# Two joined transformer-style blocks in float32 on one core: SBUF tiles moved to 2048-byte offsets, the compression's position column merged into its matmuls, and all weights packed in the order in which they are loaded

## What is computed

```python
def compress(t, j):                      # keys (j = 0) and values (j = 1)
    blk = t[:, win_idx] + pe[j][None, None, :, None, :]     # 15 windows of 32 tokens, stride 16
    h = jax.nn.silu(jnp.einsum('bnlgd,ldf->bngf', blk, w1[j]))   # l = 32, d = 64, f = 128
    return h @ w2[j]
```

## Time and profile before

| | |
|---|---|
| median of the runs | 2589.13 us (2587.99 to 2589.91, 3 runs) |
| the profiled execution, its own time | 2592.49 us |
| its span | 2590.7 us |
| mean granted TensorE clock | 0.948 |
| PE busy (matmul / weight load) | 2344.5 us (90%) / 1926.3 us (74%) |
| DVE, ACT busy | 1672.1 us (65%), 1098.6 us (42%) |
| transfers | 531.24 MB, 205 GB/s over the span; 208080 of 293659 packets under 2 KB |

### The profile page before, as it was taken

One profiled execution on the slowest core, in us unless ns is written; L12 is line 12 of the kernel. 1 busy time (PEld: TensorE's weight loads), 2 busy tenths in 40 slices (PEclk: granted clock), 3 DMA queues, 4 the chain that ended last, 5 costly groups with the idle time before them and its releaser, 6 DMA issues.

```text
span 2590.7 us, 30688 instructions
## 1 busy us (share of the span) xinstructions
PE 2344.5 (90%) x11132; PEld 1926.3 (74%) x11132; DVE 1672.1 (65%) x2111; ACT 1098.6 (42%) x1221; POOL 0.2 (0%) x4
## 2 busy tenths in 40 slices
PE   0999994899999985999999898999999989899998
PEld 0787884688788774788788686778878869677786
DVE  7677667676677776676677644577757764456444
ACT  1434634433534554443433434543444343464333
POOL 0000000000000000000000000000000000000000
PEclk9999997999999995999999987999999998799999
DMA  9787431497488540596588632248758883223552
GB/s 376 273 299 280 142 109 33 160 322 264 173 321 311 185 163 16 203 321 235 211 319 301 186 115 82 98 166 322 281 187 306 307 239 107 98 98 114 178 194 105
DMA packets 293659, 531.24 MB, mean 205 GB/s; under 512 B 14800, under 2 KB 208080, under 8 KB 275024
## 3 DMA queue, kind: packets, MB, share of 16 engines
q1 hardware_dynamic: 293584, 530.23, 58.9%
HBM read 529.12 MB, written 1.05 MB: 205 GB/s over the span
## 4 chain that ended last, share of the span: by engine, by line
PE 80%; DVE 10%; ACT 5%; issue 2%; DMA 2%; SPq 1%; DVEq 0%; ACTq 0%
PE GU L1391 14%; PE GU L1393 14%; PE GU L1395 14%; PE PY L1391 9%; PE PY L1393 9%; PE PY L1395 9%; DVE wL L810 2%; ACT wH L490 2%; PE TM L1441 1%; PE PY L1409 1%; PE PY L1693 1%; PE PY L1591 1%; PE PY L1688 1%; DMA M<-in_ada_t 1%; DVE M L817 1%
## 5 line engine op out<-in xcount | busy, mean ns | idle before, releaser
L810 DVE TENSOR_TENSOR wL<-raw,wH 128x2048 fp32r<-128x2048 f32 x352 | 794.6, 2279 | 331.0 <-ACT wH L490 330.5
L490 ACT ACTIVATE wH<-raw 128x2048 fp32r<-128x2048 f32 x352 | 659.3, 1899 | 216.9 <-PE PY L1395 101.7
L1391 PE MATMUL GU<-wH,xH 128*128 128x512 f32 (+1 forms) x1600 | 642.3, 401 | 35.0 <-DVE xL L898 16.7
L1393 PE MATMUL GU<-wL,xH 128*128 128x512 f32 (+1 forms) x1600 | 631.2, 394 | 0.0
L1395 PE MATMUL GU<-wH,xL 128*128 128x512 f32 (+1 forms) x1600 | 630.7, 394 | 0.0
L1391 PEld LDWEIGHTS GU<-wH,xH 128*128 128x128 f32 x1600 | 302.3, 189 | 107.3 <-issue 35.9
L553 ACT ACTIVATE hH<-TM 128x512 fp32r<-128x512 f32 x88 | 52.7, 599 | 715.7 <-PE TM L1441 715.7
L1395 PEld LDWEIGHTS GU<-wH,xL 128*128 128x128 f32 x1600 | 302.1, 189 | 71.6
L1393 PEld LDWEIGHTS GU<-wL,xH 128*128 128x128 f32 x1600 | 302.7, 189 | 65.8
L817 DVE CUSTOM_DVE_ANT_0 ada<-ada,cond 128x1024 f32<-128x1024 f32 x256 | 298.1, 1220 | 0.0
L1391 PE MATMUL PY<-wH,hH 128*128 128x512 f32 x704 | 224.2, 399 | 27.0 <-DVE hL L911 27.0
(11 more groups left out here) (278 smaller groups left out, 2074.6 us busy)
## 6 DMA issues: line engine op xcount, KB each, us to landing
ada<-in_ada_t SPq DMA_DIRECT2D x128, 1024.0 KB, 8.0
raw<-in_ffn_wi SPq DMA_DIRECT2D x176, 512.0 KB, 5.8
raw<-in_ffn_w_in SPq DMA_DIRECT2D x176, 512.0 KB, 5.6
raw<-in_ffn_wo SPq DMA_DIRECT2D x88, 512.0 KB, 4.4
raw<-in_ffn_w_out SPq DMA_DIRECT2D x88, 512.0 KB, 4.3
raw<-in_mix_w_in SPq DMA_DIRECT2D x64, 512.0 KB, 4.5
M<-in_ada_t SPq DMA_DIRECT2D x16, 1024.0 KB, 10.4
raw<-in_a_w_in SPq DMA_DIRECT2D x32, 512.0 KB, 4.5
```

The lines of the kernel that those rows point to most:

```text
L490: act.activation(wH[:, slot, 0:words], raw[:, slot, 0:words], ACT.Copy).then_inc(s_high, 1)
L810: dve.tensor_tensor(wL[:, slot, 0:words], raw[:, slot, 0:words], wH[:, slot, 0:words], ALU.subtract).then_inc(s_split, 1)
L1391: pe.matmul(outs[i], aH, wh[i], start=first, stop=False)
L1393: pe.matmul(outs[i], aH, wl[i], start=False, stop=False)
```

## The change

1. **Layout.** A tile `pad` of 480 floats comes first, `M` moves ahead of `cst`, `acc` goes to the end. Then `raw`, `wH`, `wL`, `ada`, `x`, `xn`, `xH`, `xL`, `hH`, `hL`, `sh`, `gB`, `M` and `cst` all start at a multiple of 2048 bytes. The order and size of the instructions do not depend on it.
2. **Compression.** `cT_` is laid out anew as (j, 8, 34): for each of 8 positions 32 columns (2 groups by 16) and two of `pe`, which a new DVE copy puts there. One product of 33 contiguous columns does windows and `pe` column together. ACT fills `cT_` with four copies in place of two.
3. **Weights.** The host packs every piece as 128 rows of 2048 contiguous floats. For the feed-forwards a piece is one block; for the mixers a partition's row holds all pieces of that mixer, one behind the other (16, 20 or 26 of them). Each transfer now reads runs of 1024 floats (4 KB). `w1` is two transfers of 1 MB over 128 partitions with runs of 2048 floats, the MLP's matrix has runs of 1024. `w2` and the broadcasts are as before.

```diff
+        sb("pad", [P, 480])
         raw = sb("raw", [P, RING, PIECE])
...
         gB = sb("gB", [P, D])
+        M = sb("M", [P, ARENA])
         cst = sb("cst", [P, C_END])
...
-            def load(view, k0, nk, lo, width):
+            def load(src, words=PIECE):
 
                 slot = t.next("piece") % RING
                 sp.wait_ge(s_split, t.next(s_split))
-                dst = raw[:, slot, 0:nk * width].rearrange("p (k n) -> p k n", k=nk)
-                for q in range(2):
-                    sp.dma_start(dst[:, q * nk // 2:(q + 1) * nk // 2, :],
-                                 view[:, k0 + q * nk // 2:k0 + (q + 1) * nk // 2, lo:lo + width]
-                                 ).then_inc(s_raw[slot], 16)
+                for g in range(2):
+                    half = slice(g * words // 2, (g + 1) * words // 2)
+                    sp.dma_start(raw[:, slot, half], src[:, half]).then_inc(s_raw[slot], 16)
...
                     for k in range(2):
-                        for two in range(2):
-                            sp.dma_start(w1_[k].rearrange("p (l f) -> p l f", f=P)[two * 64:(two + 1) * 64],
-                                         T["cmp_w1_2"][i, k].rearrange("(l two) d f -> two d l f", two=2)[two]
-                                         ).then_inc(s_w1, 16)
+                        sp.dma_start(w1_[k], T["cmp_w1"][i, k]).then_inc(s_w1, 16)
...
-                src = TMf.rearrange("p (m s) -> p m s", s=S)
-                dst = cT_.rearrange("p j g s -> p (j g) s")
-                act.activation(dst[0:64], src[0:64], ACT.Copy)
-                act.activation(dst[64:P, :, 0:S - 1], src[64:P, :, 1:S], ACT.Copy).then_inc(s_aT, 1)
+                src = TMf.rearrange("p (j g q n two) -> p j two n g q", j=2, g=2, q=16, two=2)
+                for j in range(2):
+                    for two in range(2):
+                        r = slice(64 * two, 64 * two + 64)
+                        ins = act.activation(cT_[r, j, :, 0:32].rearrange("p n (g q) -> p n g q", g=2),
+                                             src[r, j, two], ACT.Copy)
+                ins.then_inc(s_aT, 1)
...
+                dve.tensor_copy(cT_[:, :, :, 32:34].rearrange("p j n h -> p j h n"),
+                                peT[:, (l - 2) * 32:(l - 1) * 32].rearrange("p (j h n) -> p j h n", j=2, h=2))
...
-                        pe.matmul(PY[:, 2, 64 * j:64 * j + 30], w, cT_[:, j, :, 2 * n:2 * n + 16 * (NCMP - 1) + 1:16],
-                                  start=(n == 0), stop=(n == 15))
-                    for n in range(16):
-                        w = w1_[j][:, n * P:(n + 1) * P]
-                        at = (l - 2) * 32 + j * 16 + n
-                        ins = pe.matmul(PY[:, 2, 64 * j + 32:64 * j + 33], w, peT[:, at:at + 1],
+                        ins = pe.matmul(PY[:, 2, 64 * j:64 * j + 33], w, cT_[:, j, n % 8, n // 8:n // 8 + 33],
                                         start=(n == 0), stop=(n == 15))
```

More of the change, by code:

```diff
@@ L63, with whole @@
 C_FREQ = C_CSIN + 32
-C_END = C_FREQ + 8
+C_END = C_FREQ + 16
 N_CONST = 2
 N_LATE = 6
+def whole(order, width=512):
+    return [(k0, lo, width) for lo in order for k0 in (0, 4)]
+PIECES_A = whole((2 * D, D, 0, 2 * D + 512, 3 * D, 3 * D + 512, D + 512, 512)) + [
+    (k0, 4 * D + lo, 512) for k0 in (0, 4) for lo in (0, 512)]
+PIECES_B = whole([h * 512 for h in range(6)]) + whole([3 * D + h * 512 for h in range(2)])
+C_IN, C_OUT = 4376, 4376 + D
+PIECES_C = (whole((512, 0)) + whole((1024,), 280) + whole((1816, 1304, 2328, 2840, 3352, 3864))
+            + [(k0, C_IN + h * 512, 512) for h in range(2) for k0 in (0, 4)]
+            + [(k0, C_OUT + h * 512, 512) for k0 in (0, 4) for h in range(2)])
 class Tally:
@@ L316, in ada_turns @@
                 return l, ADA_FIRST, ADA_REST
[L317 to L321 removed]
+            return (l + 1, 0, ADA_FIRST) if l + 1 < 4 else (l, 0, 0)
         block = ctx.enter_context(nc.Block())
@@ L328, in _, with load_mixer @@
             t = Tally()
[L330 removed]
+            def load(src, words=PIECE):
                 slot = t.next("piece") % RING
                 sp.wait_ge(s_split, t.next(s_split))
[L334 to L360 removed]
+                for g in range(2):
+                    half = slice(g * words // 2, (g + 1) * words // 2)
+                    sp.dma_start(raw[:, slot, half], src[:, half]).then_inc(s_raw[slot], 16)
+            def load_up(l, j, c, q):
+                load(T["up_w"][l, j // 2, q][bass.ds(c, 1)].rearrange("c p n -> p (c n)"))
+            def load_down(l, j, c):
+                load(T["down_w"][l, j // 2][bass.ds(c, 1)].rearrange("c p n -> p (c n)"))
+            def load_mixer(w, pieces):
+                at = 0
+                for k0, lo, width in pieces:
+                    load(w[:, at:at + 4 * width], 4 * width)
+                    at += 4 * width
             def load_start(c, q):
@@ L432, in _ @@
                     ffn(l, j)
[L433 to L448, removed]
+                elif l < 2:
+                    load_mixer(T["ab"[l] + "_w"], (PIECES_A, PIECES_B)[l])
                 else:
@@ L1871, with packed @@
     given["table"] = table()
+    def packed(w, pieces):
+        rows = w.reshape(ND, P, -1)
+        return _np.concatenate([rows[k0:k0 + 4, :, lo:lo + width].transpose(1, 0, 2).reshape(P, 4 * width)
+                                for k0, lo, width in pieces], axis=1)
+    given["up_w"] = _np.ascontiguousarray(both("ffn_wi", "ffn_w_in_2").reshape(4, 2, 2, 4, P, 2, NF, CF).transpose(
+        0, 1, 2, 6, 4, 3, 5, 7)).reshape(4, 2, 2, NF, P, PIECE)
+    given["down_w"] = _np.ascontiguousarray(both("ffn_wo", "ffn_w_out_2").reshape(4, 2, NF, 2, P, D).transpose(
+        0, 1, 2, 4, 3, 5)).reshape(4, 2, NF, P, PIECE)
@@ new lines @@
+    for name in "ab":
+        given[name + "_w"] = packed(_np.concatenate([array(name + "_w_in")[0], array(name + "_w_out")[0]], axis=1),
+                                    PIECES_A if name == "a" else PIECES_B)
+    given["c_w"] = _np.stack([packed(_np.concatenate(
+        [array("mix_w_in_2")[i], _np.concatenate([array("proj_a_2")[i], array("proj_b_2")[i]]), array("w_out_2")[i]],
+        axis=1), PIECES_C) for i in range(2)])
+    given["cmp_w1"] = _np.ascontiguousarray(array("cmp_w1_2").reshape(2, 2, 16, P, P).transpose(0, 1, 3, 2, 4)).reshape(
+        2, 2, P, PIECE)
@@ L1872 @@
+    given["gm_ws"] = _np.ascontiguousarray(array("gm_ws_2").transpose(0, 2, 1, 3)).reshape(2, P, D)
     for name, a in given.items():
```

45 lines of the change are left out of this document (16 added, 29 removed).

## The result

The changed kernel takes 2506.08 us (2504.83 to 2507.24, 4 runs) against 2589.52 us of the kernel before beside it (2587.99 to 2593.22, 4 runs): ratio 0.9676, 95% interval 0.9659 to 0.9692. That is 83.4 us less, where 47.5 was forecast. The profiled execution has a span of 2505.7 us, 85.0 less than before; its own time is 2507.24.

The account below looks back on a forecast made before the run. PE was taken to bound the kernel, 80% of the chain of waits. -27.3 - 18.9 - 1.3 = -47.5 us from 2589.1 gave 2541.6 us; own range 2534 to 2549, 8-in-10 range 2528 to 2562.

Parts of the forecast that it names:

- Compression, -27.3: Layers 2 and 3: 64 of 128 records go from each compression, saving 13.66 and 13.6 us.
- the rival that half comes back: After the compressions PE finds a cut or load not ready; 13.6 us come back, 2555.2 us; chance 0.06.
- Entries, -18.9: Entry of layers 2 and 3: faster loads ahead of the mixer's first piece remove excesses of 10.69 and 8.25 us.
- The rival: Entries of layers 2 and 3: run length is not what slows them, they give nothing; 2560.5 us, chance 0.09.
- Start, -1.3: Program start: the first three pieces load faster, saving 1.3 us; at least 0, at most 5.25.
- All other loads, 0: Loads elsewhere: the rate rises but slots are filled before PE wants them, so nothing gained.
- Layout, 0: PE's wide matmuls in steady loops: new tile offsets change nothing, distances stay 233 and 117 ns; bound 163 us either way.
- three things say no: Against layout as cause: loss proportional to columns, same rate at two offsets, no variation with the stationary tile's start.
- the rival's 163 us: Wide matmuls: the layout is what PE lost, 20 ns each; up to 163 us more gain, 2379 us; chance 0.08.
- The collision, 0.04: Wide matmuls: equal tile starts modulo 2048 cost PE a conflict; 2705 us with 20 ns each; chance 0.04.

Follow-up runs that it names:

- e3: The kernel before with the merged compression alone (64 records in place of 128): 2563.34 us, ratio 0.9900.
- e2: The changed kernel with the layout of before; merged compression and packed weights stay: 2543.93 us, ratio 0.9820.
- e8: The kernel before with only w1 and the MLP's matrix packed in long runs: 2574.23 us, ratio 0.9932.
- e1: The kernel before with the new layout alone (pad first, M ahead of the constants, acc last), loads and compression as before: 2548.52 us, ratio 0.9840.
- e10: The kernel before with one line moved: acc (16 bytes) goes behind M; no pad: 2557.64 us, ratio 0.9864.
- e12: The kernel before with the new layout alone (pad first, M ahead of the constants, acc last), run again: 2552.19 us, ratio 0.9845.
- e14: The kernel before with acc last and M ahead of the constants, no pad: 2554.04 us, ratio 0.9859.
- one grid: PE alone, no reference computed: bursts of 24 fp32r matmuls over moving and stationary offsets, some beside other engines; 226.7 ns at difference 0 for 512 columns.
- e9: PE alone, no reference computed: finer moving offsets, column counts, stationary columns and strides; 226.7 ns for 512 columns at difference 0.

## Why the prediction was right or wrong

**Compression, -27.3: right.** e3 gives 27.2 alone; in e2 the mixers of layers 2 and 3 are shorter by 13.7 and 12.9 us. What the text said of the stretch itself, 9.9 and 10.3 us, was 8.65 and 7.82 in the changed kernel. The text had 32 of the 64 records at the high clock; there it was 48 in layer 2 and 56 in layer 3, in e2 36 and 44, in e3 57 and 27. Nothing that it frees was held by ACT or a load, and the rival that half comes back is refuted.

**Entries, -18.9: right, and for the reason given.** In e2 the feed-forwards ahead are 10.7 and 8.2 us shorter, 18.9 in sum, and e8 shows that the loads of `w1` and of the MLP's matrix do it. The rival had named the small `w2`, the broadcasts or the writing beside PE and DVE; all of these stayed in e8, so it is refuted in these. The size is that of one trace: in the six other kernels that keep the old loads (e1, e3, e10, e12 to e14) the entries take 19.4 to 23.9 us where the trace of before has 23.86 and 21.42. By the rule of the Trainium skill in *DMA: Bandwidth & Descriptors*, section Specifications, 512-byte runs are at line rate and this term is zero. The traces do not agree: ahead of the mixer's first piece 184 GB/s were moved in runs of 512 bytes, and 378 GB/s in runs of 8 and 4 KB.

**Start, -1.3: right;** 1.7 in e2, 2.1 in the changed kernel.

**All other loads, 0: right.** In e2 the six feed-forwards without such an entry behind them differ from before by 0.2 us or less each, though every piece moves in longer runs.

**Layout, 0: wrong, and all of the miss.** The median is 35.5 us under the forecast, and e2 to the changed kernel, which is the layout alone, is 37.9 (on two chips). The step that failed reads "The layout could be the cause; three things say no". All three are true and none bears on it. They show that the loss does not depend on where *one* operand stands, and what counts is how the two stand to each other. Both groups compared had unequal offsets, 128 against 160 and the same pair with the roles swapped, and the stationary tile moves by 512 bytes, which leaves the difference modulo 256 as it is. The trace of before had no fp32r matmul of 512 or 256 columns with equal offsets, so it could not answer for them; "no evidence" was written as "evidence against", and 0.08 was too low a chance for it. It did hold a sign that I had not used: the 96 matmuls of 280 columns, whose blocks lie 1120 bytes apart, so that their differences were 224, 64, 160 and 0. In the second piece of each layer they took about 126, 127, 129 and 128 ns by block. So position did count, though the equal one did not stand out. The size was off as well: I put all 20 ns of loss at stake, and 5.8 of them went, so the rival's 163 us were 38. In numbers: 45.8 us at full clock; e2 to the changed kernel is 38.1 on the span, 30.5 in the feed-forwards, 7.2 in the mixers, 0.4 at the start.

The rest was given back. The 256-column matmuls took back 1.1 us. The mixers of layers 0 and 1 gain nothing from their 672 wide matmuls (3.9 us by the rate), and why is not shown. PE's waits sum to 220.6 us in the changed kernel and to 216.8 in e2. A feed-forward gains 3.6 to 4.4 us where its 792 matmuls at 5.8 ns make 4.6, and one gains only 2.1, the second of layer 2: behind its boundary the clock fell. Windows of the changed kernel and of e2 at that place (length, busy, PEclk):

```profile
1674.00:1681.00 7.00, 6.47 (x20) 5.10 (x19) 4.47 (x12) 4.19 (x11) 0.00 (x0) 0.51 0.22 63
```

```profile
1698.00:1705.00 7.00, 5.94 (x34) 4.94 (x33) 4.58 (x13) 4.28 (x12) 0.00 (x0) 1.00 0.25 62
```

0.51 against 1.00, both behind a boundary where PE waits for the norm. Why the clock fell in one and not in the other is not shown.

**The collision, 0.04: refuted with its sign turned.** "If such equal offsets cost PE a conflict": for 512 columns equal is the best of all differences tried, and for 256 columns it costs 2.8 ns on 384 matmuls.

The Trainium skill, in *TensorE: Matmul & The Clock Gate*, section "Wait — 56ns, not 53.3ns?", gives a fixed 2.5 ns over the columns' time. The fixed part is borne out in form at difference 0 from 256 columns on (13.3 ns at 512, 384 and 256 columns), not in size; at 128 columns and at other differences the excess is another.

## What to carry to other kernels

Where the distance of fp32r matmuls in the trace is above N/2.4 GHz by several per cent, look at where its *two* operands start relative to each other: here tiles that start equal modulo 256 bytes took 2.5% off every 512-column matmul at the full clock, and a 16-byte tile declared between them had cost it. Before a mechanism is ruled out from a trace, ask whether the trace contains the case that would show it; if it doesn't, give it its bounds and a fair chance, not zero. A transfer in short runs costs most for what stands behind it in the queue: 2.5 MB for `w1` and the MLP's matrix were never waited for themselves, and cost 19 us through the piece behind them.

## What the runs showed of the hardware that I had not expected

- The distance of fp32r matmuls at 2.4 GHz depends on the operands' relative start: 226.7 ns at a difference of 0 modulo 256 bytes, 228.9 at 64, 233.3 at most others, up to 240.0 at 40 (512 columns, 128 stationary). At 256 columns the order is another: difference 0 (120.0 ns) is among the slowest, 192 is at 113.3, and 64 at 113.3 in one grid and 117.8 in the other.
- A DVE subtraction, an ACT copy and loads at 119 to 152 GB/s beside it changed neither the 226.7 nor the 233.3 ns.
- Narrow matmuls with 128 stationary columns did not get shorter with their columns: 128 columns of fp32r took 111.7 ns (e9), and a record of the plain float32 matmuls in the compression took 109 to 112 ns at the full clock and 213 at the low one, with 1, 30 or 33 columns.
- At 1.2 GHz there is no excess: 426 or 427 ns for 512 columns in both kernels, twice 213.3.
- The same stretch of 64 narrow records took 7.8 us in layer 2 of e3 and 10.8 in layer 3, mostly at the full and mostly at the low clock.
